# Delta rule by chunks: the next chunk's key products and turned keys in the tail of this chunk, the output gate inside the chunk loop

## What is computed

```python
G = cumsum(g); decay = where(causal, exp(G[:, None] - G[None, :]), 0)
kb = k * beta
m = where(strict, kb @ k.T * decay, 0) + eye
u, w = triangular_solve(m, [v * beta, kb * exp(G)])
v_new = u - w @ state
out = (q * exp(G)) @ state + where(causal, q @ k.T * decay, 0) @ v_new
state = state * exp(G[-1]) + (k * exp(G[-1] - G)).T @ v_new
...
mix = sigmoid(gg) * (out * rsqrt(mean(out ** 2) + eps) * gdn_norm) * silu(z)
```

## Time and profile before

| | |
|---|---|
| median of three runs | 2987.02 us |
| the profiled execution, its own time | 2992.39 us |
| its span, first to last instruction | 2990.7 us |
| busy share PE, DVE, ACT, POOL | 84%, 39%, 29%, 20% |
| `gdn_prompt`, from about 707 to 1108 us | 401 us |
| `gdn_sample`, 1108.4 to 1183.5 us | 75 us |
| `gate_gdn`, 1183.5 to 1249.2 us | 65.7 us |

### The profile page before, as it was taken

The page is one execution under the profiler, slowest core; times in us unless marked ns, Lnnn a source line. Parts: engine busy times, 40 slices in busy tenths (PEclk is TensorE's granted clock), DMA queues, the critical chain, the costliest instruction groups (busy, mean ns, idle before and its releaser), DMA issues. The chain is left out here.

```text
span 2990.7 us, 45944 instructions
## 1 busy us (share of the span) xinstructions
PE 2510.0 (84%) x18554; PEld 1928.1 (64%) x18554; DVE 1166.1 (39%) x2034; ACT 854.8 (29%) x1813; POOL 600.9 (20%) x679
## 2 busy tenths in 40 slices
PE   5999999997888877279999997799988937999990
PEld 5999999996887873135566554555553525666660
DVE  6366652213455534434555544344431131111115
ACT  3167721201111210714444443233320101111111
POOL 0220000002243222023332221344410021000002
PEclk9999999997898875689999998899998968999995
DMA  4562232225221103710100002556615207888876
GB/s 126 174 199 85 83 105 97 90 84 166 80 76 54 51 23 116 263 62 8 37 22 23 22 22 75 207 220 243 244 74 174 95 30 281 329 318 317 326 274 243
DMA packets 163809, 412.74 MB, mean 138 GB/s; under 512 B 28371, under 2 KB 96696, under 8 KB 142729
## 3 DMA queue, kind: packets, MB, share of 16 engines
q1 hardware_dynamic: 127305, 249.94, 24.0%
q0 software_dynamic: 36320, 160.18, 14.7%
HBM read 315.05 MB, written 95.22 MB: 137 GB/s over the span
## 5 line engine op out<-in xcount | busy, mean ns | idle before, releaser
L131 PE MATMUL pi_acc<-hT_hi,pi_w_hi 128*128 128x352 f32 (+1 forms) x1152 | 378.3, 328 | 0.0
L131 PE MATMUL pi_acc<-hT_lo,pi_w_hi 128*128 128x352 f32 (+1 forms) x1152 | 371.4, 322 | 0.0
L131 PE MATMUL pi_acc<-hT_hi,pi_w_lo 128*128 128x352 f32 (+1 forms) x1152 | 371.2, 322 | 0.0
L131 PEld LDWEIGHTS pi_acc<-hT_hi,pi_w_hi 128*128 128x128 f32 x1152 | 217.2, 189 | 4.0 <-issue 3.8
L131 PEld LDWEIGHTS pi_acc<-hT_lo,pi_w_hi 128*128 128x128 f32 x1152 | 217.0, 188 | 4.0 <-issue 3.8
L131 PEld LDWEIGHTS pi_acc<-hT_hi,pi_w_lo 128*128 128x128 f32 x1152 | 216.9, 188 | 0.0
L1543 PE MATMUL at_sc<-at_keyT,at_qT 96*128 96x512 f32 (+5 forms) x480 | 162.7, 447 | 1.7 <-ACT at_val L1710 0.8
L1863 PE MATMUL as_tp<-ident,as_lat 128*128 128x128 f32 x1024 | 127.8, 279 | 25.4 <-ACT as_cT L2051 25.4
L1722 ACT ACTIVATE at_p<-at_sc,at_nm 16x16 f32<-16x16 f32 (+5 forms) x144 | 100.8, 700 | 159.9 <-DVE at_nm L1630 158.7
L1628 DVE TENSOR_REDUCE at_mx<-at_sc 16x1 f32<-16x16 f32 (+5 forms) x144 | 101.4, 704 | 99.1 <-PE at_sc L1547 98.1
L2179 PE MATMUL po_acc<-po_w,po_mix 128*128 128x512 f32 (+1 forms) x288 | 126.7, 599 | 14.1 <-DMA po_mix<-mixT 14.1
(11 more groups left out here) (471 smaller groups left out, 4727.5 us busy)
## 6 DMA issues: line engine op xcount, KB each, us to landing
ex_wg<-w_gate SPq DMA_DIRECT2D x33, 1024.0 KB
ex_wu<-w_up SPq DMA_DIRECT2D x33, 1024.0 KB
ex_wd<-w_down SPq DMA_DIRECT2D x33, 1024.0 KB
pi_piece<-w_in SPq DMA_DIRECT2D x64, 384.0 KB, 3.4
expert_out<-pi_zero POOLq DMA_DIRECT2D x33, 512.0 KB, 12.1
expert_out<-ex_y SPq DMA_DIRECT2D x33, 512.0 KB, 2.7
projT<-pi_xr POOLq DMA_DIRECT2D x24, 524.0 KB, 3.0
convT<-pi_yn POOLq DMA_DIRECT2D x24, 512.0 KB, 2.9
```

What stands on the lines that cost most here:

```text
L131: last = nc.tensor.matmul(out, lhs[a], rhs[b], start=(start and i == 0), stop=(stop and i == 2))
```

## The change

In `gdn_prompt`: kk(f+1) goes into R1 and kt(f+1) into R0, and both stand in the tail of iteration f, around m6 and yo. `gp_LT` has two buffers. DVE makes LT and ktok of chunk f+1 at the end of iteration f. The differences become eight instructions of one head each in level 1; the causal mask goes to POOL; ACT copies vtok ahead of vn. The output is no longer copied out: ACT squares it from PSUM, DVE multiplies it with the norm's weights and the gates, PE sums the squares in level 4 (into R1), ACT takes Ln in level 4 and Exp in level 5, POOL multiplies, and SP stores into `mixT`. SP loads the two gates of a chunk (512 KB each), and POOL multiplies them. `gdn_sample` gates its own output; `gate_gdn` and `gdnT` are gone.

```diff
 # SP
+                def load_gates(c):
+                    if c >= 2:
+                        sp.wait_ge(mix_stored, 16 * (c - 1))
+                    for i, at in enumerate((Z0, GG0)):
+                        sp.dma_start(zg[:, c % 2, i, :, 0:n], d["projT"][at:at + GH, :, r0:r0 + n].rearrange("h p t -> p h t")).then_inc(zg_loaded[c % 2], 16)
...
                 for c in range(NT):
                     if c + 2 < NT:
                         load_rows(c + 2)
                         load_heads(c + 2)
-                    sp.wait_ge(o_kept, c + 1)
-                    sp.dma_start(d["gdnT"][:, :, r0:r0 + n].rearrange("h p t -> p h t"), o[:, :, 0:n]).then_inc(out_stored, 16)
+                    if c:
+                        store_mix(c - 1)
+                        if c + 1 < NT:
+                            load_gates(c + 1)
                 sp.wait_ge(S_ready, NT)
...
+                store_mix(NT - 1)
+                sp.wait_ge(mix_stored, 16 * NT)
 # PE
+                def key_products(c):
+                    wait_heads(pe, c)
+                    if c >= 2:
+                        pe.wait_ge(logged, c - 1)
...
+                    for h in range(GH):
+                        last = nc.tensor.matmul(R1[0:n, h, 0:n], kk[:, h, :], kk[:, h, :], start=True, stop=True)
+                    last.then_inc(kk_done, 1)
+                def key_rows(c):
+                    if c >= 2:
+                        pe.wait_ge(S_ready, c - 1)
...
+                    for h in range(GH):
+                        last = nc.tensor.transpose(R0[0:n, h, :], kk[:, h, :], k.ident[:])
+                    last.then_inc(kt_done, 1)
...
                     if back:
                         pe.wait_ge(kg_made, b + 1)
+                        if go:
+                            pe.wait_ge(ktok_kept, f + 1)
...
                     if go:
+                        pe.wait_ge(lt_made, f + 1)
+                        for h in range(GH):
+                            last = nc.tensor.transpose(R1[0:n, h, :], v[:, h, :], k.ident[:])
+                        last.then_inc(vt_done, 1)
+                        if f:
+                            pe.wait_ge(xy_kept, 2 * BU[f])
+                            pe.wait_ge(m_kept, 2 * MU[f])
+                        if f >= 2:
+                            pe.wait_ge(m6_kept, f - 1)
+                            pe.wait_ge(yo_kept, f - 1)
                         for h in range(GH):
                             last = nc.tensor.matmul(I1[0:n, h, 0:n], kk[:, h, :], q[:, h, :], start=True, stop=True)
...
+                    def sums():
+                        pe.wait_ge(o_kept, b + 1)
+                        for h in range(0, GH, H2):
+                            last = nc.tensor.matmul(R1[:, h:h + H2, 0:nb], k.ones[:], sq[:, h:h + H2, 0:nb], start=True, stop=True)
+                        last.then_inc(summed, 1)
...
+                        if l == 4 and back:
+                            sums()
...
+                    if f + 1 < NT:
+                        key_products(f + 1)
                     if f:
                         pe.wait_ge(m_kept, 2 * MU[f + 1])
                         pe.wait_ge(xy_kept, 2 * BU[f + 1])
...
                         last.then_inc(m6_done, 1)
+                    if f + 1 < NT:
+                        key_rows(f + 1)
+                    if f:
                         pe.wait_ge(m6_kept, f)
 # DVE
-                    nc.vector.tensor_tensor(mine, rows[0:n, c % 2, 0, :, 0:n], k.G[0:n, c, :].unsqueeze(2).to_broadcast([n, GH, n]), ALU.subtract).then_inc(diffed, 1)
-                    nc.vector.tensor_scalar(mine, mine, 0.0, None, ALU.min).then_inc(limited, 1)
+                    for h in range(GH):
+                        last = nc.vector.tensor_scalar(decay[0:n, h, 0:n], rows[0:n, c % 2, 0, h, 0:n], k.G[0:n, c, h:h + 1], 0.0, ALU.subtract, ALU.min)
...
+                    def keep_out():
+                        dve.wait_ge(squared, b + 1)
+                        dve.wait_ge(zg_made, b + 1)
+                        nc.vector.scalar_tensor_tensor(out=mine, in0=R1[:, :, 0:nb], scalar=k.vecT[:, V_GDN:V_GDN + 1], in1=mine, op0=ALU.mult, op1=ALU.mult).then_inc(o_kept, 1)
...
-                        if l == LV[f] - 3 and f + 1 < NT:
+                        if l == 1 and f + 1 < NT:
+                            dve.wait_ge(attn_made, f + 1)
                             difference(f + 1)
-                        if l == LV[f] - 1 and f + 1 < NT:
-                            mask(f + 1)
+                        if l == 2 and back:
+                            keep_out()
+                        if l == LV[f] - 2 and f + 1 < NT:
+                            scale(f + 1)
+                    if f + 1 < NT:
+                        lower(f + 1)
+                        keep_keys(f + 1)
                     if f:
                         dve.wait_ge(yo_done, f)
 # POOL, in this order: level 0, level 1, kg(f), gates(b), level 2, qg(f), level 3, decayed(f), level 4, mask(f+1), level 5, mix(b)
+                    def gates():
+                        pool.wait_ge(zg_loaded[b % 2], 32 * (b // 2 + 1))
+                        nc.gpsimd.tensor_tensor(mine, mine, zg[:, b % 2, 1, :, 0:nb], ALU.mult).then_inc(zg_made, 1)
+                    def mix():
+                        pool.wait_ge(rooted, b + 1)
+                        pool.wait_ge(o_kept, b + 1)
+                        nc.gpsimd.tensor_tensor(mine, mine, sq[:, :, 0:nb], ALU.mult).then_inc(mixed, 1)
 # ACT
-                        nc.scalar.copy(o[:, :, 0:nb], R1[:, :, 0:nb]).then_inc(o_kept, 1)
+                        nc.scalar.activation(sq[:, :, 0:nb], R1[:, :, 0:nb], ACT.Square).then_inc(squared, 1)
+                        nc.scalar.activation(sq[:, :, 0:nb], R1[:, :, 0:nb], ACT.Ln, bias=k.eps[:], scale=1.0 / DK).then_inc(logged, 1)
+                        nc.scalar.activation(sq[:, :, 0:nb], sq[:, :, 0:nb], ACT.Exp, scale=-0.5).then_inc(rooted, 1)
...
 # gdn_sample, DVE
+                V.tensor_tensor(zg[:, 0], zg[:, 0], zg[:, 1], ALU.mult).then_inc(gated, 1)
...
+                V.scalar_tensor_tensor(out=oT[:], in0=oT[:], scalar=k.vecT[:, V_GDN:V_GDN + 1], in1=zg[:, 0], op0=ALU.mult, op1=ALU.mult).then_inc(gated, 1)
...
+                    if g == 2:
+                        V.tensor_tensor(oT[:], oT[:], sq[:], ALU.mult).then_inc(gated, 1)
 # decoder_step
-        gate_gdn(k)
```

More of the change, by code:

```diff
@@ L720, in size @@
+        b_made, kg_made, qg_made, decayed_made, zg_made, mixed = (s.sem(f"gp_{n}") for n in (
+            "b_made", "kg_made", "qg_made", "decayed_made", "zg_made", "mixed"))
         def size(c):
@@ L806, in _ @@
                     if go:
+                        n = size(f)
+                        q, kk, v = (qkv(f, i) for i in range(3))
+                        pe.wait_ge(lt_made, f + 1)
[8 more added lines that the diff above has]
+                            pe.wait_ge(yo_kept, f - 1)
                         for h in range(GH):
@@ L909, in mask, with lower, keep_keys @@
                     last.then_inc(scaled_made, 1)
+                def lower(c):
+                    dve.wait_ge(kk_done, c + 1)
+                    dve.wait_ge(scaled_made, c + 1)
+                    for p0, p1, c0, c1 in halves(c):
+                        last = nc.vector.tensor_tensor(LT[p0:p1, c % 2, :, 0:c1 - c0], R1[p0:p1, :, c0:c1], scaled[p0:p1, :, 0:c1 - c0], ALU.mult)
+                    last.then_inc(lt_made, 1)
+                def keep_keys(c):
+                    n = size(c)
+                    dve.wait_ge(kt_done, c + 1)
+                    nc.vector.tensor_tensor(ktok[0:n, c % 2], R0[0:n], k.left[0:n, c, :].unsqueeze(2).to_broadcast([n, GH, P]), ALU.mult).then_inc(ktok_kept, 1)
                 nc.vector.memset(Y[:], 0.0)
@@ L916, in _ @@
                 difference(0)
-                mask(0)
+                scale(0)
+                lower(0)
+                keep_keys(0)
                 for b in range(-1, NT):
@@ L920, in _ @@
                     go, back = f < NT, b >= 0
-                    if go:
-                        n = size(f)
-                        dve.wait_ge(kk_done, f + 1)
-                        dve.wait_ge(scaled_made, f + 1)
-                        for p0, p1, c0, c1 in halves(f):
-                            last = nc.vector.tensor_tensor(LT[p0:p1, :, 0:c1 - c0], I0[p0:p1, :, c0:c1], scaled[p0:p1, :, 0:c1 - c0], ALU.mult)
-                        last.then_inc(lt_made, 1)
                     if back:
@@ L1017, in _ @@
                     nc.gpsimd.tensor_tensor(qg[:, f % 2, :, 0:n], qkv(f, 0), row_exp[:, :, 0:n], ALU.mult).then_inc(qg_made, 1)
-                    for l in range(3, LV[f]):
-                        level(l)
+                    level(3)
+                    if f:
+                        pool.wait_ge(S_ready, f)
+                    else:
+                        pool.wait_ge(zeroed, 1)
```

(26 more changed lines are left out.)

236 lines of the change are left out of this document (95 added, 141 removed).

## The result

The changed kernel takes 2901.93 us (median of four runs, 2897.44 to 2904.31); the kernel before, run beside it, takes 2990.02 (2985.99 to 2993.04). The ratio is 0.9704, with a 95% interval of 0.9685 to 0.9724: some 88 us less. The profiled execution took 2902.68 us, with a span of 2901.0. Against the profiled one of before (2992.39) that is 89.7 less, where the sum said 82.

The account below looks back on a forecast made before the run. A gating stage standing alone, and PE at chunk boundaries (waits, then low clock), bound the kernel. -65.7 - 37 - 5 + 14 + 9 + 3 = -82 us gives 2910 against the profiled execution, 2905 at the median's level; range 2884 to 2940.

Parts of the forecast that it names:

- Gating stage, loop's end, sample: Separate stage removed, -65.7 us; uncovered gating chain after the last outputs, +9; three small DVE products in sample stage, +3.
- Boundary: Between full chunks, key products and turned keys fill PE's tail: 18.97 to 13.65 us, 5.3 gained, seven times, -37.
- spread differences: DVE's differences and ACT's exponentials moved from level 3 to level 1: 7 x 0.7 = -5 us.
- The reason given for the clock: At the boundary PE's idle stretch lowers the clock to 0.50; without that stretch it stays at 1.00, gaining 5.3 us.
- PE's issue: Five PE waits, 10.5 us, in stretches of loads; may vanish or double: 0, between -10.5 and +10.5.
- Sums: Sums on PE in level 4, with no gap to hide them: +2.0 us in seven iterations, +14.
- Second rival: DVE and POOL obstruct each other: two path instructions, 1.1 us more each, eight iterations, +18, so 2923; chance 0.14.
- a sign of being wrong: On DVE: r times beta or the first xy taking above 1.6 us would show the prediction wrong.
- third rival: Same conflict uncovered: 13 SBUF-only DVE instructions per chunk lose 1.1 us each, 117 in all, 3022, slower; chance 0.03.
- First boundary: Boundary from the chunk of 16 tokens: nothing taken, between the full 5.3 us gain and a loss of 3.
- another of the prediction's signs: In the tail: PE waiting at ks for ktok would show the prediction wrong.
- The forecast of -30: Seven full chunks: -37 for boundaries, -5 for spread differences, +12 for the six sums lying there.

Follow-up runs that it names:

- new order alone: Against the changed kernel: output copy, its store, the loads behind it and the gating stage as in the kernel before; 2952.21 us, 0.9874.
- gating alone: Against the changed kernel: kk at the iteration's start in I0, kt behind qk in R1, ktok and vn as before; 2938.09 us, 0.9828.
- moved loads alone: Against the kernel before: SP issues chunk c-1's store in iteration c, so loads no longer wait for the output copy; 2976.07 us, 0.9952.
- gate product later: Against the changed kernel: GpSimd's gate product issued after its level 2 product instead of before it; 2894.73 us, 0.9697.
- loads put back: Against the changed kernel: row and head loads of chunk c+2 wait for chunk c-1's squares; 2911.5 us, 0.9754.

## Why the prediction was right, and where its terms were off

The forecast was 2905 in 2884 to 2940; 2901.9 came, by the mechanism named. That it came within 3 us is in part luck: 14.6 us gained at the loads and 3.7 in the last chunk, by a clock that no term held, stand against 4.0 lost at the start and some 7 at a conflict of DVE and POOL.

- **Gating stage, loop's end, sample.** -65.7, +9 and +3 came as -65.7, +8.8 and +3.0. These were sums of rows.
- **Boundary.** 13.65 us was right with nothing beside it (13.2 in the new order alone), and 14.1 in the changed kernel, with a wait of 0.87. The gain of 5.3 was read off one boundary and held in two ways: some 5 by the gating alone, 6.5 with the spread differences by the order alone (5.3 + 0.7 was forecast). The 0.7 by itself was not measured.
- **The reason given for the clock** was too simple. I took the price of a full clock "since the fall of the clock followed PE's idle stretch, and that stretch goes". One wait of 1.6 us leaves the clock at 1.00; two waits lower it in six of seven tails. The step held because more than the first wait went; the second and the third were not put back by themselves.
- **PE's issue.** The term of 0, between -10.5 and +10.5, is the one that was most off. All five waits went, and with them the low clock behind: the six chunks with loads took 268.7 us before, 14.6 more than six times 42.34. In the kernel before, the moved loads alone gave 15.9 us. The prediction saw that the waits "fall in stretches of loads" and that the loads would come in two groups; it had no row to decide on. The DMA view, with the instruction packet ahead of each wait, could have been one.
- **Sums.** +2.0 a chunk was 1.71 when doubled: the term is right to within 2 us in seven chunks.
- **Second rival** (DVE and POOL). It was true in small: one wait of 0.87 us in each of seven chunks, worth 1.04 of period where nothing else waits. That is 5.3 us in the trace and 7.2 between the medians, where its price was 18. r times beta slowed down too, from 1.60 to 2.19 us in the mean, which the prediction had named as a sign of being wrong; PE does not wait for it, and with the gate product later it still takes 2.33 and the wait of 0.87 is gone. (The third rival's 117 us should be 114: 13 x 1.1 in eight chunks.)
- **First boundary.** I took 0, with a loss of up to 3. In every kernel with the new order ks waits there for some 1.6 us: mask on POOL (until 730.86 us), scale, LT and ktok on DVE run one after the other, ktok ends at 736.56 and ks starts at 736.66. PE at ks for ktok was another of the prediction's signs. What it costs is not separated: the stretch takes 48.97 us in the changed kernel, 45.9 to 48.4 in the runs that keep this order and 46.3 in the gating alone, which has no such wait (45.01 before). Part of it is clock: in the three kernels that take 48.4 to 49.0 it falls to 0.50 at 745 us, in the others at 749.8 us or later, and the state's update takes 3.66 us in the changed kernel's trace, 2.05 in that of the new order alone.
- **The sum.** The full chunks by measured terms: 7 x -6.5 for the order with the spread, -14.6 for the loads, 10.9 for the sums, 7 x 1.04 for the conflict: -45.5 - 14.6 + 10.9 + 7.3 = -41.9, against -38.4 in the table. With 5 from the gating alone and the 0.7 that was forecast it is -36.3; the table lies between. The forecast of -30 missed it by the loads, less the conflict.

## What to carry to other kernels

Before costing a change in the order of one engine, look at what else moves with it: here a store that moved in SP's program also moved the loads behind it, and that was worth as much as the sums cost. When an engine waits for "issue" beside heavy loads, look in the DMA view for instruction packets, and count the engine's records between the stops: here they were multiples of 256, and spreading the loads took all five away. An instruction added to GpSimd costs what the VectorE instructions beside it lose, and only those with both operands in SBUF lost here, so it belongs beside the others.

## What was not expected of the hardware

A single wait of 1.6 us in a busy stretch did not lower TensorE's clock, and two waits of 1.7 and 0.7 us with 1.1 us of work between them went with a fall to 0.50, in six of seven tails. A wait of 2.05 us in a stretch of short products did so too (loads put back), yet one of 2.70 in the new order alone, at 882 us, left it at 1.00: the length of one wait does not tell. And beside loads whose data it was not yet reading TensorE ran out of instructions: 1.4 to 2.6 us a time in the kernel before, up to 3.0 in the new order alone.
